# Sample mLSTM of a hybrid decoder step: decay and outer product joined in one VectorE operation per sample, GpSimd's products given up

## What is computed

```
m_new = max(logf + m, i)
decay = exp(logf + m - m_new);  w = exp(i - m_new)
C_new = decay * C + w * outer(k, v)
n_new = decay * n + w * k
h     = (q . C_new) / max(|q . n_new|, exp(-m_new))
```

## Time and profile before

| | us |
|---|---|
| median of 3 runs | 3344.78 (3342.7 to 3346.07) |
| profiled execution | 3348.81 |
| its span | 3347.0 |
| PE busy | 3070.3 (92%) |
| DVE busy | 1266.8 (38%) |
| ACT busy | 978.6 (29%) |
| POOL busy | 343.4 (10%) |
| mean granted PE clock | 0.947 of full speed |

### The profile page before, as it was taken

One profiled execution on the slowest core, in us unless ns is written; L12 is line 12 of the kernel. 1 busy time (PEld: TensorE's weight loads), 2 busy tenths in 40 slices (PEclk: granted clock), 3 DMA queues, 4 the chain that ended last, 5 costly groups with the idle time before them and its releaser, 6 DMA issues.

```text
span 3347.0 us, 49333 instructions
## 1 busy us (share of the span) xinstructions
PE 3070.3 (92%) x19991; PEld 2876.7 (86%) x19991; DVE 1266.8 (38%) x1979; ACT 978.6 (29%) x1657; POOL 343.4 (10%) x342
## 2 busy tenths in 40 slices
PE   5999959989999999999888688988789999999999
PEld 5999838889999999998787577776379999999999
DVE  5112753443322323342031677775054332232332
ACT  4212414332211111131323576664042321111110
POOL 0000120000100101000000243442000100000010
PEclk8999979899999999999889698998889999999999
DMA  4110043011111111112400000001321111111113
GB/s 147 57 45 20 1 146 127 26 38 44 50 46 49 42 53 44 41 47 75 142 32 20 1 1 1 1 1 59 94 82 38 44 50 45 44 49 46 48 45 129
DMA packets 64341, 173.37 MB, mean 52 GB/s; under 512 B 7473, under 2 KB 28095, under 8 KB 63055
## 3 DMA queue, kind: packets, MB, share of 16 engines
q1 hardware_dynamic: 49512, 153.18, 13.8%
q10 hardware_dynamic: 14664, 17.90, 1.7%
HBM read 157.25 MB, written 17.99 MB: 52 GB/s over the span
## 4 chain that ended last, share of the span: by engine, by line
PE 71%; DVE 6%; ACT 3%; issue 2%; DVEq 2%; SPq 2%; DMA 1%; POOL 0%; POOLq 0%; ACTq 0%
PE ps L348 58%; PE ps L2396 1%; PE ps L1880 1%; PE ps L2353 1%; PE ps L2340 1%; PE ps L1453 1%; PE ps L2695 1%; PE ps L2342 1%; SPq L1850 1%; DVE jf L2507 0%; SPq L1851 0%; PE ps L1175 0%; PE ps L1420 0%; DVEq L2262 0%; PE ps L1446 0%
## 5 line engine op out<-in xcount | busy, mean ns | idle before, releaser
L348 PE MATMUL ps<-h_hi,w_hi 128*128 128x344 f32 x3360 | 727.3, 325 | 50.4 <-DVE h_lo L407 12.1
L348 PE MATMUL ps<-h_lo,w_hi 128*128 128x344 f32 x3360 | 720.7, 323 | 0.0
L348 PE MATMUL ps<-h_hi,w_lo 128*128 128x344 f32 x3360 | 716.4, 322 | 0.0
L348 PEld LDWEIGHTS ps<-h_hi,w_hi 128*128 128x128 f32 x3360 | 572.7, 190 | 58.3 <-issue 45.2
L348 PEld LDWEIGHTS ps<-h_lo,w_hi 128*128 128x128 f32 x3360 | 575.8, 191 | 0.0
L348 PEld LDWEIGHTS ps<-h_hi,w_lo 128*128 128x128 f32 x3360 | 567.1, 190 | 0.0
L300 DVE TENSOR_TENSOR w_lo<-w_raw,w_hi 128x1024 fp32r<-128x1024 f32 (+1 forms) x202 | 302.7, 1500 | 299.6 <-ACT w_hi L294 299.4
L294 ACT ACTIVATE w_hi<-w_raw 128x1024 fp32r<-128x1024 f32 (+1 forms) x202 | 208.5, 1033 | 491.0 <-PE ps L348 431.0
L1653 POOL TENSOR_TENSOR f_silu<-f_silu,nb_r 128x1032 f32<-128x1032 f32 x44 | 106.6, 2423 | 1756.2 <-ACT f_silu L1617 1756.2
L1575 DVE TENSOR_TENSOR xT<-xT,ps 128x1032 f32 (+1 forms) x64 | 78.7, 1229 | 448.9 <-PE ps L348 448.9
L348 PE MATMUL ps<-hid_hi,w_hi 128*128 128x344 f32 x1056 | 223.9, 320 | 0.0
(11 more groups left out here) (496 smaller groups left out, 3676.1 us busy)
## 6 DMA issues: line engine op xcount, KB each, us to landing
w_raw<-w_gu SPq DMA_DIRECT2D x88, 512.0 KB, 3.6
w_raw<-w_dn SPq DMA_DIRECT2D x32, 448.0 KB, 3.2
w_raw<-w_a SPq DMA_DIRECT2D x27, 512.0 KB, 3.7
xT<-xT SPq DMA_DIRECT2D x2, 4128.0 KB, 16.0
w_raw<-w_o SPq DMA_DIRECT2D x16, 512.0 KB, 3.7
w_raw<-w_dn SPq DMA_DIRECT2D x16, 512.0 KB, 3.7
pages<-cmp SPq DMA_DIRECT2D x64, 128.0 KB, 2.5
w_raw<-w_b SPq DMA_DIRECT2D x9, 512.0 KB, 3.6
```

Of the source, the lines that this page charges most:

```text
L348: mm = pe.matmul(ps[:, 3 * slot + c, 0:cut], w[:, slot, k * P:(k + 1) * P], a[:, k, c * cut:(c + 1) * cut], start=(k == 0 and w is w_hi an ...
```

## The change

POOL's eight products are gone. In `added(n)` DVE waits for the part's load and for the outer products, and then runs eight scalar_tensor_tensor, one for each sample: state = state * decay + outer product, 192 columns, with the decay as a per-partition scalar from `smb` and the outer product read from PSUM. The last of the eight increments `cs_w`.

```diff
         def samples_pool(pool):
-            for n in range(8):
-                h = n // 2
-                _, p0, r = parts(h)[n % 2]
-                if n:
-                    pool.wait_ge(e_dec, n)
-                pool.wait_ge(cs_in[n % 4], 16 * (n // 4 + 1))
-                c3 = cs[n % 4][p0:p0 + r, :].rearrange("p (b e) -> p b e", b=NB)
-                pool.tensor_tensor(c3, c3, smb[p0:p0 + r, h, NB:2 * NB].unsqueeze(2).to_broadcast([r, NB, DH]),
-                                   ALU.mult).then_inc(e_dec, 1)
             pool.wait_ge(e_f, 2)
             pool.tensor_tensor(s_rr[:, :], s_rr[:, :], nhalf[0:NB, :], ALU.pow).then_inc(e_g, 1)
...
             def added(n):
                 _, p0, r = parts(n // 2)[n % 2]
-                dve.wait_ge(e_dec, n + 1)
+                dve.wait_ge(cs_in[n % 4], 16 * (n // 4 + 1))
                 dve.wait_ge(e_kv, n + 1)
-                c4 = cs[n % 4][p0:p0 + r, :].rearrange("p (b e) -> p b e", b=4)
-                dve.tensor_tensor(c4, c4, ps[p0:p0 + r, 0:4, 0:2 * DH], ALU.add).then_inc(cs_w, 1)
+                for b in range(NB):
+                    state = cs[n % 4][p0:p0 + r, b * DH:(b + 1) * DH]
+                    ins = dve.scalar_tensor_tensor(out=state, in0=state,
+                                                   scalar=smb[p0:p0 + r, n // 2, NB + b:NB + b + 1],
+                                                   in1=ps[p0:p0 + r, b // 2, (b % 2) * DH:(b % 2 + 1) * DH],
+                                                   op0=ALU.mult, op1=ALU.add)
+                ins.then_inc(cs_w, 1)
```

## The result

The changed kernel ran in 3340.28 us (median of 20 runs, 3332.77 to 3347.97) against 3347.11 us for the kernel before on the same chips (20 runs, 3341.85 to 3353.32): a ratio of 0.9981, 95% interval 0.9973 to 0.9988, or 6.4 us at the centre (the two medians are 6.8 apart). The forecast was -6.9. The centre lies just on the "no difference" side of the 0.2% line that the forecast sat on; that it is faster at all is clear of the interval.

A forecast was written before the change was run, and what follows sets the result against it. In the stage, DVE held by POOL's products bounds the preparation, then TensorE, then the last part's load chain. Net -8.9 + 2.0 = -6.9 us, from 3344.78 to 3337.9 us; range 3334 to 3344.

The forecast's parts named there:

- The start, 8.9 us: Preparation before the loop: without POOL's products holding DVE, `added(0)` starts at 440.65 instead of 449.54, 8.9 us gained.
- Rival 4: Preparation: DVE's long operations were slow for a reason other than POOL, first gain nil; +2.0, 3346.8 us, chance 0.04.
- A = 2.68: DVE's eight small operations of one state part: 7 x 0.325 + 0.40 = 2.68 us in place of 1.75.
- Rivals 1 (3.29) and 2 (1.75): DVE's additions: every small operation held, 3342.3 us, chance 0.11; or per-instruction cost hidden, 3334.5 us, chance 0.05.
- DVE becomes the bound, round 3.80: Loop: a DVE round of 3.80 us exceeds TensorE's 3.58; two steps with a `spread` take 4.42.
- A + 1.12: Loop round: DVE's additions plus 0.06 to TensorE and 1.06 from outer product to next addition.
- The loads cost nil: Loop: loads 4 to 7, 7.37 us each, land before DVE's additions want them, so they cost nothing.
- Rival 5: Loop: a load comes one us later than its slack allows, costing one us; about 3340 us, chance 0.06.
- the covers: Loop: slack between each state load's landing and its wanted time, between zero and 2.6 us.
- The loop, 2.0 lost: From the start of `added(0)` to the end of dots 7: 35.4 us instead of 33.4, 2.0 lost.
- Rival 3: Loop: TensorE, waiting for DVE, falls back to 1.2 GHz; 6 to 14 us lost, say 3355 us, chance 0.04.
- The absolute time, 3337.9: Whole kernel: median of the runs shown, 3344.78 us, less the net 6.9, gives 3337.9 us.

The follow-up runs named there:

- two-pass run: Changed kernel with each eight scalar_tensor_tensor replaced by two DVE passes over 1536 columns, decay product then addition; one execution, 3350.18 us.
- both together: Changed kernel with semaphores between DVE and TensorE counted by PSUM bank, plus useless TensorE matmuls (8, then 3 behind the denominators); ratio 0.9962, median 3336.90 us.

## Why the prediction was right

Its steps, in its order:

1. *The start, 8.9 us.* Right to a tenth: `added(0)` starts 5.70 after the `vw_all` subtraction, 14.59 before, so 8.89. The mechanism, two engines taking turns, was argued from neighbouring rows; the run with POOL later (preparation short although the products are there) and the run with POOL kept busy (14.1, although its products serve nothing) show it in both directions. Rival 4 falls.
2. *A = 2.68.* Measured 2.69, and 2.79 for parts 3 and 7, the ones that begin on partition 64. Rivals 1 (3.29) and 2 (1.75) fall. Of the Trainium skill's sentence in VectorE: DVE Perf Modes, "The DRAIN you can't avoid", by which the next operation waits for the pipeline to empty, this trace shows the exception it allows: 0.40 recorded each, 0.327 apart.
3. *DVE becomes the bound, round 3.80.* The two steps with a `spread` are 4.45 (from 452.87) and 4.34 (from 461.24), 4.42 forecast; the others are 3.92, 3.80 and 3.82. The two runs that change A alone move the end as the rule A + 1.12 says: down to TensorE's 3.60 with 1.75, up to 4.73 with 3.59.
4. *The loads cost nil.* Right: no operation on `cs` waits for a DMA in the changed kernel. Rival 5 falls. One landing in the working is off by its own terms: 461.1 + 7.37 is 468.5, not 468.8, and the covers then run from zero to 2.7; nothing hangs on it.
5. *The loop, 2.0 lost.* It lost 2.6 (33.4 to 36.05). The mis-sized term is the slow first round, taken as 5.83 from the rows of before and measured as 6.29 (6.33 in the second profile); the two parts with 2.79 add 0.2. The rest is 0.1 or less in any step. So the stage gained 6.3 and not 6.9. That the two medians are 6.8 apart, nearly the forecast, is luck, since the interval is 5 us wide.
6. *Rival 3, the clock falls back while TensorE waits for DVE.* It did not decide here, but it was no empty rival: in the run with POOL kept busy, whose loop is the change's, and in the two-pass run it happened. In the former the loop took 38.1 against 36.05, 2.1 us more, although its first round was 0.6 shorter. The chance of 0.04 was small for what two of the runs then showed in part.
7. *The absolute time, 3337.9.* It was 3340.28, inside the range of 3334 to 3344. The miss of 2.4 us is nearly all the starting point: the forecast counted from the median of three runs, 3344.78, and twenty runs of the kernel before have 3347.11. The range allowed 1.7 us for that at one end and nothing at the other.

## What to carry to other kernels

Before a product on a helper engine is called free because that engine is idle, look at what the other engine does in those microseconds: here the first four POOL products of 2.75 lay beside DVE operations with two SBUF inputs and held them up by 8.9 us, twice the 4.4 that the same work costs the loop on DVE. Moving them by one wait gave as much as the whole change. And where two engines hand a set of banks to and fro, the sum of both is the round (2.69 and 1.12 here, 3.8); counting the semaphores by bank hid the shorter side, and the round was TensorE's 3.6.

## What was not expected of the hardware

TensorE's clock in this stage does not follow how early TensorE gets work. Where it rose from 1.2 to 2.4 GHz, counted from the start of the stage: 22 us in both profiles of the change, 22 with POOL later, 22 with useless matmuls from 7 us on, 22 with the handshake by bank, alone and with the matmuls, 19.6 in the run without decay, 21 with two passes, 29 before and 29 with POOL kept busy. Counted from outer product 1 that is 3.6 us (POOL later) to 8.0 us (both together). What sets this moment stays open; so does why the clock fell once in a loop in which it held in the two profiles of the change. The first round took 6.29 in the change, where a later one takes 3.8, so 2.5 us of the stage are still lost there, and in every version it took 5.25 or more.
